# Expert units of eight jobs in one order through the change of jobs, with gather and scatter placed among the units

## The chip, the cores and the metric

One core of one Trainium2 chip runs the whole program. The metric is the device time of the slowest (here the only) core in microseconds; what is compared is the median of several runs. PE is TensorE, PEld its weight loads, DVE is VectorE, ACT is ScalarE, POOL is GpSimd, SP is SyncE, which issues the weight loads from memory.

## What is computed

One step of a two-layer encoder over 288 tokens (256 of a prompt, 32 of a sample) with D = 1024. Each layer is a mixer (gated MLP, banded attention, short convolution, merged) and a feed-forward part: dense in layer 0, a mixture of eight experts with top-2 routing in layer 1. The change touches only the mixture and what follows it:

```python
def swiglu(h, w1, w3, w2):
    a = jnp.einsum('...d,df->...f', h, w1)
    g = jnp.einsum('...d,df->...f', h, w3)
    return jnp.einsum('...f,fd->...d', jax.nn.silu(a) * g, w2)

def moe(h, w_router, b_router, w1, w3, w2):
    logits = jnp.einsum('...d,de->...e', h, w_router) + b_router
    top_v, top_i = lax.top_k(logits, TOP_K)          # 2 of 8
    top_w = jax.nn.softmax(top_v, axis=-1)
    combine = jnp.einsum('...k,...ke->...e', top_w, jax.nn.one_hot(top_i, N_EXPERTS))
    return sum(combine[..., e:e+1] * swiglu(h, w1[e], w3[e], w2[e]) for e in range(N_EXPERTS))
```

An expert has an inner width of 3584. A final RMSNorm over the sum follows. All inputs and outputs are float32.

## The kernel before

Every product in full precision is made of three products in the rounded format float32r: with w = w_hi + w_lo and h = h_hi + h_lo, the kernel adds h_hi*w_hi, h_hi*w_lo and h_lo*w_hi. ScalarE makes a high part by a copy with rounding (round_chunk, L873), VectorE the low part by subtraction (low_chunk, L1338). A weight matrix of 128 x 2048 (1 MB) comes by one DMA from SP into one of six slots (expert_ring) and is split in two chunks of 128 x 1024; there are four buffers w_hi and w_lo (CHUNKS = 4). ScalarE may round chunk c when TensorE has used chunk c - 4 (semaphore chunk_used); VectorE follows (rounded), TensorE waits for split; SP loads the next matrix into a slot when both its chunks are split.

The experts run as jobs. A job is one expert with up to 128 of its tokens (SLOT), and in the profiled execution there are eight, so one per expert. A job has 14 units (UNITS) of 256 inner columns. For each unit TensorE does unit_rows (four chunks, 24 matmuls of 128x512, L1682 to L1684; the out tile holds w1 and w3 columns side by side), ScalarE the SiLU of one half (silu_unit, L881), VectorE the product (silu_times_g, L1343), TensorE two transposes of the result (transpose_hidden, L1692), ScalarE and VectorE its high and low part (hid_high L885, hid_low L1347), and TensorE unit_down (two chunks, 12 matmuls, L1708), which adds into the PSUM banks 6 and 7 over all units of a job. The down projection of a unit comes one unit later, behind the next unit's unit_rows, so that SiLU, transposes and splitting are hidden. Only the job's first unit has no down projection in front of its transposes, and the job's last down projection comes right after its own transposes.

At the two ends of a job stand other steps, all in the function job_units of each engine. Ahead of unit 0, two matmuls with a column of zeros clear banks 6 and 7 (L1720). Behind the last down projection TensorE makes three transposes of the weighted one-hot matrix (L1739), then gather (L1662) for the next job: 24 matmuls of float32 that pick the next job's tokens out of h_tok by the one-hot matrix spread, in tiles of 128, 128 and 32 tokens (a float32 matmul stands as two passes in the trace). ScalarE and VectorE take high and low part of it (L720, L1353), which the next unit_rows needs. ScalarE copies the sums to y_tok (L933), and the scatter follows: eight float32 matmuls of 288 columns (L1747) whose results VectorE adds to x (L1414). These steps use a rotation of the PSUM banks 0 to 5. While they run, ScalarE and VectorE split only the first four chunks of the next job, since there are four buffers.

The order on each engine is written out by hand; there is no scheduler. The loop over the jobs (Fori) covers all but the last one, which is written out again; in it a loop over turns of two units covers twelve of the fourteen. VectorE loads two expert numbers into registers at the loop's head. The end of the program is the last scatter, the squares of x, mean(4), root and norm, and the output DMA from POOL.

## Times and profile before

| | us |
|---|---|
| median of three runs | 1971.55 |
| lowest, highest | 1969.06, 1981.17 |
| profiled execution: its device time | 1977.98 |
| profiled execution: span of its instructions | 1976.2 |
| PE busy in the span | 1882.6 (95%) |
| DVE busy | 1440.9 (73%) |
| ACT busy | 1170.9 (59%) |
| mean granted TensorE clock | 0.976 |
| first expert matmul to last down matmul of job 7 | 869.97 to 1951.36 |

Busy time of PE counts pipelined matmuls whose ends are modelled, each longer than the distance to the next, so 95% doesn't say that PE is at its peak: the distance between starts says more. A row of the timeline gives start, length, engine, line, operation, tiles, shapes and count, and in brackets how long the engine was idle ahead of it and which instruction ended that. Register and branch instructions are in no row.

### The profile page before, as it was taken

How to read it: one execution, taken by the hardware profiler on the slowest of the kernel's cores; microseconds unless marked ns; L12 is line 12 of the kernel's file. 1: busy time of each engine (PE TensorE's matmuls, PEld its weight loads, DVE VectorE, ACT ScalarE, POOL GpSimd, SP SyncE). 2: the span in 40 equal slices, each digit the busy share in tenths (PEclk: the TensorE clock that was granted, in tenths of full speed). 3: DMA queues.
4: the chain of work that ended last, by engine and by line, in shares of the span. 5: the costliest groups of instructions: out<-in, count | busy, mean ns of one | idle time of the engine just before them, and what ended most of it. 6: DMA issues, size and time to landing. Idle time of an engine off the chain costs nothing.

```text
span 1976.2 us, 31336 instructions
## 1 busy us (share of the span) xinstructions
PE 1882.6 (95%) x10698; PEld 1653.7 (84%) x10698; DVE 1440.9 (73%) x1909; ACT 1170.9 (59%) x1522; POOL 19.7 (1%) x39
## 2 busy tenths in 40 slices
PE   7999998999899999889999999999999999999996
PEld 6999998999799999768878778778788787787785
DVE  5563565666655645459979979789799799798896
ACT  4453434333436344348868768678688587686784
POOL 1000000000000000000000000000000000000000
PEclk8999999999999999979999999999999999999999
DMA  7444543444344344329969969879799699698792
GB/s 281 142 161 147 180 162 110 169 152 174 126 162 142 112 146 167 132 87 373 363 240 373 365 236 374 307 291 368 262 361 375 231 373 371 232 372 330 290 371 85
DMA packets 67991, 478.95 MB, mean 242 GB/s; under 512 B 7840, under 2 KB 8864, under 8 KB 10704
## 3 DMA queue, kind: packets, MB, share of 16 engines
q1 hardware_dynamic: 65168, 467.82, 63.4%
q0 software_dynamic: 2608, 10.08, 1.5%
q8 instruction: 51, 0.84, 0.2%
q14 instruction: 20, 0.16, 0.0%
q10 hardware_dynamic: 144, 0.04, 0.0%
HBM read 474.23 MB, written 3.69 MB: 242 GB/s over the span
## 4 chain that ended last, share of the span: by engine, by line
issue 67%; PE 29%; DVE 2%; ACT 1%; DMA 0%; POOL 0%; SPq 0%; ACTq 0%; POOLq 0%; DVEq 0%
PE psum L1584 9%; PE psum L1586 9%; PE psum L1585 9%; DVE h L976 1%; DMA ring<-in_w_in 0%; PE psum L1464 0%; PE psum L1463 0%; DVE rstd L973 0%; DVE w_lo L986 0%; PE psum L1483 0%; ACT w_hi L686 0%; PE psum L1453 0%; DVE attn L1154 0%; PE psum L1525 0%; ACT L716 0%
## 5 line engine op out<-in xcount | busy, mean ns | idle before, releaser
L1338 DVE TENSOR_TENSOR w_lo<-ring,w_hi 128x1024 fp32r<-128x1024 f32 x448 | 543.4, 1224 | 71.5 <-ACT w_hi L873 47.0
L873 ACT ACTIVATE w_hi<-ring 128x1024 fp32r<-128x1024 f32 x448 | 476.1, 1065 | 116.6 <-PE psum L1684 83.5
L986 DVE TENSOR_TENSOR w_lo<-ring,w_hi 128x1024 fp32r<-128x1024 f32 x218 | 266.5, 1224 | 268.1 <-ACT w_hi L686 268.1
L686 ACT ACTIVATE w_hi<-ring 128x1024 fp32r<-128x1024 f32 x218 | 230.9, 1061 | 380.2 <-PE psum L1586 378.5
L1584 PE MATMUL psum<-h_hi,w_hi 128*128 128x288 f32 x1312 | 395.9, 302 | 33.7 <-DVE h_lo L992 22.9
L1585 PE MATMUL psum<-h_lo,w_hi 128*128 128x288 f32 x1312 | 390.8, 298 | 0.0
L1586 PE MATMUL psum<-h_hi,w_lo 128*128 128x288 f32 x1312 | 389.4, 297 | 0.0
L1682 PE MATMUL psum<-w_hi,h_hi 128*128 128x512 f32 x896 | 365.0, 407 | 0.8 <-issue 0.2
L1684 PE MATMUL psum<-w_hi,h_lo 128*128 128x512 f32 x896 | 354.5, 396 | 0.0
L1683 PE MATMUL psum<-w_lo,h_hi 128*128 128x512 f32 x896 | 353.8, 395 | 0.0
L1338 DVE TENSOR_TENSOR w_lo<-spare,w_hi 128x1024 fp32r<-128x1024 f32 x224 | 274.0, 1225 | 24.3 <-ACT w_hi L873 6.0
L1584 PEld LDWEIGHTS psum<-h_hi,w_hi 128*128 128x128 f32 x1312 | 249.4, 190 | 40.9 <-issue 33.9
L873 ACT ACTIVATE w_hi<-spare 128x1024 fp32r<-128x1024 f32 x224 | 237.8, 1062 | 66.5 <-PE psum L1684 66.5
L1586 PEld LDWEIGHTS psum<-h_hi,w_lo 128*128 128x128 f32 x1312 | 250.4, 191 | 0.0
L1585 PEld LDWEIGHTS psum<-h_lo,w_hi 128*128 128x128 f32 x1312 | 250.0, 191 | 0.0
L1682 PEld LDWEIGHTS psum<-w_hi,h_hi 128*128 128x128 f32 x896 | 171.3, 191 | 38.6 <-issue 6.3
L1684 PEld LDWEIGHTS psum<-w_hi,h_lo 128*128 128x128 f32 x896 | 170.9, 191 | 37.4
L1683 PEld LDWEIGHTS psum<-w_lo,h_hi 128*128 128x128 f32 x896 | 171.8, 192 | 33.0
L1708 PE MATMUL psum<-w_hi,hid_hi 128*128 128x512 f32 x448 | 138.9, 391 | 8.1 <-DVE hid_lo L1347 8.1
L1708 PE MATMUL psum<-w_hi,hid_lo 128*128 128x512 f32 x448 | 138.3, 390 | 0.0
L1708 PE MATMUL psum<-w_lo,hid_hi 128*128 128x512 f32 x448 | 138.1, 390 | 0.0
L1708 PEld LDWEIGHTS psum<-w_hi,hid_hi 128*128 128x128 f32 x448 | 83.5, 188 | 26.7 <-issue 9.9
(230 smaller groups left out, 1959.5 us busy)
## 6 DMA issues: line engine op xcount, KB each, us to landing
ring<-in_e_w SPq DMA_DIRECT2D x224, 1024.0 KB, 4.9
spare<-in_e_w SPq DMA_DIRECT2D x112, 1024.0 KB, 4.8
ring<-in_w_in SPq DMA_DIRECT2D x56, 1024.0 KB, 4.9
ring<-in_w SPq DMA_DIRECT2D x33, 1024.0 KB, 4.8
ring<-in_w_branch SPq DMA_DIRECT2D x12, 1024.0 KB, 4.8
ring<-in_w_out SPq DMA_DIRECT2D x8, 1024.0 KB, 4.8
bias<-in_bias_t POOLq DMA_DIRECT2D x2, 1024.0 KB, 9.9
x<-in_x_t SPq DMA_DIRECT2D x4, 288.0 KB, 3.8
```

The lines of the kernel that those rows point to most:

```text
L686: nc.scalar.activation(dst, src, ACT.Copy).then_inc(rounded, 1)
L873: nc.scalar.activation(w_hi[buf][:, :], expert_ring[s][:, half * CHUNK_W:(half + 1) * CHUNK_W], ACT.Copy).then_inc(rounded, 1)
L976: ins = nc.vector.scalar_tensor_tensor(out=h[:, k, :], in0=x[:, k, :], scalar=vec[:, gain + k:gain + k + 1], in1=rstd[:, :], op0=ALU.mult, ...
L986: nc.vector.tensor_tensor(low, src, high.bitcast(f32), ALU.subtract).then_inc(split, 1)
L1338: nc.vector.tensor_tensor(w_lo[buf][:, :], expert_ring[s][:, half * CHUNK_W:(half + 1) * CHUNK_W], w_hi[buf][:, :].bitcast(f32), ALU.subtr ...
L1584: nc.tensor.matmul(bank(name), high, high_src[k], start=(k == 0), stop=False)
L1585: nc.tensor.matmul(bank(name), high, low_src[k], start=False, stop=False)
L1586: ins = nc.tensor.matmul(bank(name), low, high_src[k], start=False, stop=(k == tiles - 1))
L1682: nc.tensor.matmul(out, he_hi[:, k, :], w_high, start=(k == 0), stop=False)
L1683: nc.tensor.matmul(out, he_hi[:, k, :], w_low, start=False, stop=False)
L1684: ins = nc.tensor.matmul(out, he_lo[:, k, :], w_high, start=False, stop=(k == DT - 1))
L1708: ins = nc.tensor.matmul(psum[:, 6 + hf, :], h_part[:, b, :], w_part[:, hf * 512:(hf + 1) * 512], start=False, stop=(last and h_part is hi ...
```

## The change

It takes effect from the end of the routing on. The parts:

- **One order through the change of jobs.** Each matrix stream is now w13, w13, w2 for every unit, with w2 being that of the unit before (np.roll), the one of the last unit wrapping to the front of the next job. Turns are of two units, seven per job; the first two and the last are written out, four run in a loop. In turn 0 of a job TensorE does unit_rows(0), then unit_down of the job before. Job 0 and the last job are written out; the very last down projection stands behind the loops.
- **Gather in the last turn.** In the last turn, after the transposes of unit 12 and ahead of unit_rows of unit 13, TensorE gathers for the next job, from h_tok_hi into banks 4 and 5 and from h_tok_lo into banks 0 and 2, in float32r: 48 matmuls in place of 24 in float32. ScalarE and VectorE copy them to he_hi and he_lo after unit_rows of unit 13. VectorE makes h_tok_lo once, ahead of job 0 (six instructions), and TensorE waits for it.
- **Scatter in four pairs.** ScalarE scales the sums by the token weights while it rounds them (sums_high), VectorE makes the low part (sums_low), both in turn 0 of the next job. The eight rows are scattered in pairs in float32r, 16 matmuls: rows 0, 1 and 2, 3 and 4, 5 and 6, 7 at four places of turns 0 and 1, each pair through banks 4 and 5, with the addition to x on VectorE between its chunks.
- **Weights.** The one-hot matrix is turned unweighted in turn 1 (turn_spread), with three one-column matmuls for the weight of each slot. wspread, its six VectorE operations and the clearing matmuls go.
- **PSUM banks** are fixed: gated 0, 1; transposed 2, 3; 4 and 5 for the rest; sums 6, 7, cleared by start=True at the job's first down projection.

```diff
 TensorE
-            def job_units(job, is_last):
-                pe.wait_ge(he_ready, job * 2 + 2)
-                for hf in range(2):
-                    nc.tensor.matmul(psum[:, 6 + hf, :], zero_col[:, :], he_hi[0:1, 0:4, :], start=True, stop=False)
-                unit_rows("first", 0)
-                transpose_hidden("first")
-                with pe.Fori(0, TURNS) as i:
...
-                unit_rows("last", JOB_MATRICES - 4)
-                unit_down("next", JOB_MATRICES - 2)
-                transpose_hidden("last")
-                unit_down("last", JOB_MATRICES - 1)
...
-                gather("gather", 1 if is_last else 4)
...
+            def gather(after):
...
+                for source, banks in ((h_tok_hi, GATHER_HI), (h_tok_lo, GATHER_LO)):
+                    for hf in range(2):
+                        if after and source is h_tok_lo:
+                            pe.wait_ge(*((e_prod_ready, turns.unit(0)), (e_lo_ready, turns.unit(0)))[hf])
+                        for j in range(4):
+                            at = (4 * hf + j) * P
+                            for n, (t0, rows) in enumerate(TILES):
+                                ins = nc.tensor.matmul(psum[:, banks[hf], j * P:(j + 1) * P], source[0:rows, n, at:at + P],
+                                                       spread[0:rows, n, :], start=(n == 0), stop=(n == 2))
+            def scatter(*rows):
...
+                for j in rows:
+                    if j >= 2:
+                        pe.wait_ge(x_ready, turns.value(MIXER_SUMS + j - 1 - DT * back, DT))
+                    out, cols = psum[:, SPARE[j % 2], 0:TOK], slice(j * P, (j + 1) * P)
+                    nc.tensor.matmul(out, y_hi[:, cols], spread_t, start=True, stop=False)
+                    nc.tensor.matmul(out, y_lo[:, cols], spread_t, start=False, stop=True).then_inc(scattered, 1)
+            def turn_work(t, last=False):
...
+                if t == 1 and boundary:
+                    scatter(2, 3)
+                unit_rows(0)
+                if boundary or t:
+                    unit_down(4, 1, last=(t == 0))
+                turn_hidden(0)
+                if t == TURNS - 1 and not last:
+                    gather(1)
+                if t == 1 and boundary:
+                    scatter(4, 5)
+                unit_rows(1)
+                if t < 2 and boundary:
+                    scatter(*((0, 1) if t == 0 else (6, 7)))
+                unit_down(10, 0, first=(t == 0))
+                turn_hidden(1)
+                if t == 1:
+                    turn_spread()
 VectorE
+            def turn_work(t, e, following=None, last=False):
...
+                if t == 1 and boundary:
+                    add_rows(2, 3)
+                if not (turns.first and t == 0):
+                    low_chunks(4, 5)
+                low_chunks(6)
+                silu_times_g(0)
+                low_chunks(7, 8, 9)
+                if t == 0:
+                    if boundary:
+                        sums_low()
+                    nc.vector.tensor_copy(wsel[:, :], weight[:, :, bass.ds(e, 1)].rearrange("p n o -> p (n o)")
+                                          ).then_inc(wsel_ready, 1)
+                hidden_low(0)
+                if t == 1 and boundary:
+                    add_rows(4, 5)
+                low_chunks(10, 11)
+                if not last:
+                    low_chunks(12)
+                if t == TURNS - 1 and not last:
+                    gathered_low(0, 1)
+                silu_times_g(1)
+                if t == TURNS - 1 and not last:
+                    gathered_low(1, 1)
+                if not last:
+                    low_chunks(13)
+                if boundary and t < 2:
+                    add_rows(*((0, 1) if t == 0 else (6, 7)))
+                if not last:
+                    low_chunks(14, 15)
+                hidden_low(1)
+                if t == 1:
+                    turned_spread()
+                    if following:
+                        hot_rows(*following)
...
+            with dve.Fori(1, last_job) as job:
+                turns.job = job
+                job_work(expert_of(job), (job + 1, expert_of(job + 1)))
 ScalarE
+            def turn_work(t, last=False):
...
+                round_chunks(7, 8, 9)
+                if t == 0 and not turns.first:
+                    sums_high()
+                hidden_high(0)
...
+                silu_unit(1)
+                if t == TURNS - 1 and not last:
+                    gathered_high(1)
```

## Rows read from the trace of the kernel before

**Rows 1.** Windows: stretch, its length, busy PE/PEld/DVE/ACT/POOL, PEclk, DMA share, GB/s

```profile
1145.00:1282.00 137.00, 133.91 (x602) 108.23 (x602) 118.25 (x133) 101.78 (x118) 0.00 (x0) 0.99 0.85 321
1190.00:1198.40 8.40, 8.40 (x39) 6.93 (x38) 7.92 (x10) 6.93 (x8) 0.00 (x0) 1.00 1.00 376
```

**Rows 2.** Timeline of PE: starts of job 0, its end, two clearings, the last end

```profile
869.97 0.79 PE L1682 MATMUL psum<-w_hi,h_hi 128*128 128x512 f32 x1
...
995.76 0.56 PE L1739 MATMUL psum<-ident,pt 128*128 128x128 f32 x3
...
1145.88 0.73 PE L1720 MATMUL psum<-h_hi,zero_col 1*128 1x512 f32 x2
...
1283.02 0.73 PE L1720 MATMUL psum<-h_hi,zero_col 1*128 1x512 f32 x2
...
1951.36 0.56 PE L1739 MATMUL psum<-ident,pt 128*128 128x128 f32 x3
```

**Rows 3.** Timeline of PE: hidden transposes, five units apart

```profile
1181.56 0.38 PE L1692 MATMUL psum<-ident,h 128*128 128x128 f32 x2
...
1223.67 0.38 PE L1692 MATMUL psum<-ident,h 128*128 128x128 f32 x2
```

**Rows 4.** Timeline of PE: the last down projection, turned weights, gather, scatter

```profile
1267.15 0.72 PE L1708 MATMUL psum<-w_hi,hid_hi 128*128 128x512 f32 x2 [1.01 <-DVE hid_lo L1347]
...
1270.01 0.56 PE L1739 MATMUL psum<-ident,pt 128*128 128x128 f32 x3
1270.50 8.51 PE L1662 MATMUL psum<-a_t,rows 128*128 128x128 f32 x48
1278.94 4.15 PE L1747 MATMUL psum<-c_t,bias 128*128 128x288 f32 x16
```

**Rows 5.** Around the first unit's transposes: timelines of ACT and PE, a window

```profile
1289.19 1.28 ACT L881 ACT_TABLE_LOAD   x1
...
1291.38 0.69 PE L1692 MATMUL psum<-ident,h 128*128 128x128 f32 x2 [1.95 <-DVE h L1343]
...
1291.90:1294.60 2.70, 2.70 (x7) 2.15 (x7) 2.70 (x8) 0.38 (x1) 0.00 (x0) 0.50 0.74 261
```

**Rows 6.** Timeline of PE: neighbours in the rounded format, 288 columns

```profile
500.03 0.29 PE L1586 MATMUL psum<-hid_hi,w_lo 128*128 128x288 f32 x1
500.16 0.30 PE L1584 MATMUL psum<-hid_hi,w_hi 128*128 128x288 f32 x1
```

**Rows 7.** Timeline of PE inside the gather: passes on 32 rows, then on 128

```profile
1271.14 0.48 PE L1662 MATMUL psum<-a_t,rows 32*128 32x128 f32 x2
...
1271.77 0.50 PE L1662 MATMUL psum<-a_t,rows 128*128 128x128 f32 x3
```

**Rows 8.** Groups by line: weight loads of rounded and of float32 matmuls

```profile
L1708 PEld LDWEIGHTS psum<-w_lo,hid_hi 128*128 128x128 f32 x448 | 84.1, 188 | 17.5
...
L1662 PEld LDWEIGHTS psum<-a_t,rows 128*128 128x128 f32 (+1 forms) x396 | 53.7, 188 | 16.1 <-ACT rows L720 1.0
```

**Rows 9.** Timelines of DVE and ACT: chunks, low parts, sums, x, hot rows

```profile
859.83 4.63 DVE L1338 TENSOR_TENSOR w_lo<-ring,w_hi 128x1024 fp32r<-128x1024 f32 x4 [1.71 <-ACT w_hi L873]
...
1266.59 0.42 DVE L1347 TENSOR_TENSOR hid_lo<-psum,hid_hi 128x256 fp32r<-128x256 f32 x1 [0.76 <-ACT hid_hi L885]
...
1270.21 1.08 ACT L933 ACTIVATE bias<-psum 128x512 f32<-128x512 f32 x2 [0.32 <-PE psum L1708]
...
1275.45 0.69 DVE L1353 TENSOR_TENSOR h_lo<-psum,h_hi 128x512 fp32r<-128x512 f32 x1 [1.96 <-ACT h_hi L720]
...
1280.28 3.30 DVE L1414 TENSOR_TENSOR x<-x,psum 128x288 f32<-128x288 f32 x8
1286.48 3.95 DVE L1338 TENSOR_TENSOR w_lo<-ring,w_hi 128x1024 fp32r<-128x1024 f32 x3 [2.90 <-ACT w_hi L873]
...
1293.32 0.84 DVE L1331 TENSOR_SCALAR a_t<-slot_id,job_base,place 128x128 f32<-128x128 f32 x3
```

**Rows 10.** Timeline of PE: the gather of job 0

```profile
858.90 8.51 PE L1662 MATMUL psum<-a_t,rows 128*128 128x128 f32 x48 [0.68 <-ACT rows L720]
```

More of the change, by code:

```diff
@@ L197, in add @@
             self.at[n] = (b, self.total, list(self.last[b]))
[L198 removed]
+            self.last[b] = [n]
             self.total += counted([n])
[L201 to L210 removed]
 def number_groups():
@@ new lines, in round_chunks, with silu_unit @@
+            def round_chunks(*chunks):
+                at = turns.turn
+                for c in chunks:
+                    round_chunk(c)
+                    turns.turn = at
+            def silu_unit(odd):
+                act.wait_ge(chunk_used, turns.chunk(9 if odd else 3))
+                if not (turns.first and turns.turn == 0 and not odd):
+                    act.wait_ge(e_prod_ready, turns.unit(odd, 1))
+                nc.scalar.activation(e_silu, psum[:, GATED[odd], 0:UNIT], ACT.Silu).then_inc(e_silu_ready, 1)
@@ L1677, in unit_rows, with split_chunk @@
+            def split_chunk(c):
+                pe.wait_ge(split, turns.chunk(c))
+                return w_hi[turns.buffer(c)], w_lo[turns.buffer(c)]
+            def unit_rows(odd):
+                if turns.turn or not turns.first:
+                    pe.wait_ge(e_prod_ready, turns.unit(odd, 2))
+                out = psum[:, GATED[odd], :]
                 for part in range(4):
-                    hi, lo = split_chunk(at + part // 2, part % 2, in_turn)
+                    hi, lo = split_chunk(6 * odd + part)
@@ new lines, in turn_work @@
+            def turn_work(t, last=False):
+                turns.turn = t
+                boundary = not turns.first
+                if t == 1 and boundary:
[15 more added lines that the diff above has]
+                    turn_spread()
@@ new lines, in job_work @@
+            def job_work(last=False):
+                pe.wait_ge(he_hi_ready, turns.value(2, 2))
+                pe.wait_ge(he_lo_ready, turns.value(2, 2))
+                for t in range(PEELED):
+                    turn_work(t)
+                with pe.Fori(0, TURNS - PEELED - 1) as i:
+                    turns.i = i
+                    turn_work(PEELED)
+                    turns.i = None
+                turn_work(TURNS - 1, last)
+            gather(0)
+            job_work()
+            turns.first = False
@@ L1755, in _ @@
+            unit_down(4, 1, last=True)
+            scatter(*range(DT))
             mean(4)
```

602 lines of the change are left out of this document (265 added, 337 removed).

## The prediction

> **What bounds the kernel now.** First the windows, to see which engine has room. In one expert job of the kernel before, TensorE is busy for nearly all of 137 us, VectorE for 118, ScalarE for 102, and the loads run at 321 GB/s; inside a job they run at 376 GB/s with the DMA engines at share 1.00 [rows 1]. Busy time of TensorE says little, so the second view is where its instructions start. Jobs repeat every 1283.02 - 1145.88 = 137.14 us [rows 2]. Inside a job the hidden transposes of successive units stand (1223.67 - 1181.56)/5 = 8.42 us apart [rows 3], with no wait between. Fourteen units at that pace are 117.9 us, so each job loses 19.2 us at its two ends, and eight jobs have about 154 us of it. All that the change can win lies there.
>
> The order of time at one change of jobs shows where it lies [rows 4]. The last down projection waits 1.0 us for its own hidden rows. It is over at 1270.01, and then come three transposes (0.5 us), the gather (8.4 us), the scatter (4.1 us) and the clearing of the sums (0.7 us, rows 2): 13.7 us without an expert matmul. The other 5.5 us are inside the job: 137.1 - 117.9 - 13.7. They come from the first unit, which has no down projection to hide its SiLU behind: TensorE sits idle for 1.95 us, and in the stretch after that its granted clock is 0.50, the 1.2 GHz level, for some 2.7 us [rows 5].
>
> **The pieces, one by one.**
>
> *Steady units.* The new turn has the same order on every engine (two down chunks, four gated chunks, SiLU after the third, high part after the sixth), so its pace stays 8.42 us: 112 units are 943.0 us.
>
> *First and last unit.* Job 0 still starts without a down projection. It took 995.76 - 869.97 = 125.8 us to its last down matmul [rows 2], 7.9 more than 117.9; 1.3 of that is the wait before the last down projection (1.0 and the restart), which now stands only at the end of job 7. So 7.9 us stay, once. Between jobs both vanish: the last down projection runs behind the next job's first unit. The matmuls with zeros go.
>
> *Gather.* It had 24 fp32 matmuls of 128 columns in two passes, 8.4 us. It gets 48 matmuls in the rounded format (24 on the high part, 24 on the low). Their price is not in the trace, since every rounded matmul there has 288 or 512 columns: at 288 they start 0.13 us apart [rows 6], with 288/2.4 GHz = 0.12. The fp32 passes of the gather tell what 128 columns cost [rows 7]: passes on the same 128 rows start 0.11 us apart ((0.50 - 0.27)/2), but around each tile of 32 rows the gaps are 0.21 ((1271.77 - 1271.14)/3). Four gaps in six are of that kind, as if the load there came after the pass before and not under it. An fp32 pass streams two cycles a column (128 columns 0.107), so the load is about 0.1 too. A rounded matmul here has 0.053 of streaming and 0.107 of load, and in the pattern 128, 128, 32 rows with one pass each, every one sits beside a change of rows: 0.16 us each, 48 make 7.7 us. From below, with loads hidden, 128/2.4 GHz + 0.013 (what 288 columns take over 0.12) = 0.067 each, 3.2 us. From above, each as dear as the fp32 one: twice 8.44, 16.9 us. I take 7.7.
>
> Weight loads have the same duration in the two formats, 188 ns [rows 8], which speaks against the lower end. The Trainium skill, "TensorE: Matmul & The Clock Gate", section "Weight-path perf modes — Fast Weight Load (FWL) and DoubleRow", says that a full load of 128 weights takes a faster path when the input type isn't FP32. If the rounded type counted as such, the gather would be 3.2 us and not 7.7, and the result that of rival 1; the trace, with equal loads, does not agree.
>
> The gather lies behind nothing: it goes in whole on TensorE. Its evacuations lie beside the down projection of 12 x 0.227 = 2.7 us: ScalarE has 2 x 0.5 us for the high part, VectorE 2 x 0.7 us for the low one, between chunk 12 and the product (the old subtraction took 0.69, rows 9). They are ready after about 2.6 us, before the next job's rows ask for them at 3.0, so no stall; were both engines late by a chunk, 1.1 us.
>
> *Scatter.* 16 rounded matmuls of 288 columns at 0.13 = 2.1 us, instead of 4.1.
>
> *Turned weights.* Three transposes 0.5 us [rows 4], plus three fp32 matmuls of one column, six passes bounded by 0.11 and 0.21 [rows 7]: 0.9. Together 1.4 us in each of eight jobs.
>
> *The wait this brings.* VectorE now splits chunks straight through the boundary. Between them it carries sums_low (2 x 0.7), eight row additions (3.30 for eight), hot_rows (0.8) and three small copies (0.7 together, an estimate from the 0.69 of a 512-column one) [rows 9]. Back to back it needs (4.63 - 1.22)/3 = 1.14 us a chunk, and 0.4 each for product and hidden low part: 7.6 us a unit against 8.42. Over a whole job it has room (14 x 7.6 + 8 = 114 us), but not in turn 0.
>
> I follow that turn, with zero at the first matmul of the new job's unit 0. VectorE's hidden_low of the last unit comes at 3.1 (the gathered parts, then three chunks at 1.14). Then stands the loop's head with two value loads, which are in no row; before, VectorE was free from 1283.58 to 1286.48 and was released by ScalarE [rows 9], so the head costs 0 to 2.9 us. I take 1.5, the middle. Chunk 4 starts at 4.5 and is split at 5.8, where TensorE wants it at 5.5: 0.4 lost. VectorE then has ten chunks (4 to 13), two products, sums_low, wsel and hidden_low: 11.4 + 0.8 + 1.4 + 0.1 + 0.4 = 14.1, to 18.6, and rows 0 and 1 at 19.0 and 19.4. TensorE needs rows, down, transposes, rows, scatter(0, 1), down and transposes: 5.5 + 0.4 + 2.7 + 0.2 + 5.5 + 0.5 + 2.7 + 0.2 = 17.7, with 0.1 before down(10), whose chunk is queued behind sums_low. So scatter(2, 3), which waits for rows 0 and 1 to leave their banks, is 1.4 late; add_rows(0, 1) is queued behind chunk 13, and everything later of TensorE behind the scatter. Turn 1 repeats this with more room, 0.3 at turn_spread, which waits for row 7. With 0.3 for restarts that is 2.5 us per boundary. The bounds: 0.5, if the head costs nothing and the four chunk buffers take up the rest; 6, if the head costs 2.9 and one activation table is reloaded on ScalarE ahead of the rounding, as now (1.28, rows 5).
>
> *Loads.* The SP queue issues the same 42 matrices per job into the same six slots, w2 of the last unit now among the next job's. Each is asked for when its slot's second chunk is split, as before, so POOL's queue is passed by nothing. 42 x 1.049 MB = 44.0 MB at 376 GB/s are 117 us, under the 131.6 that a job will have: hidden.
>
> *Start.* VectorE makes six low parts of h_tok (6 x 0.65 = 3.9 us) before TensorE may gather, which started at 858.90 [rows 10]; so it starts 3 us later. It is 0.8 shorter, and what follows it (0.6 + 0.7 + zeros 1.2, to 869.97) shrinks by 1.6. TensorE is then idle for 3.7 us, so part of the gather may run at 1.2 GHz, as the matmuls after the idle time of rows 5 did: 0.7 (nothing to 4). Together +1.3.
>
> *End.* Before: turned weights, gather 2.1, scatter 4.1. After: high and low sums exposed (0.3 + 0.5 + 2 x 0.7 = 2.2), then eight rows through two banks, the addition of 0.41 being the pace with its waits, about 0.5 us each. 6.6 before against 6.2 after: taken as nothing.
>
> **The sum**, from the first expert matmul to the last down matmul: 943.0 + 7.9 + 7 x (7.7 + 2.1 + 2.5) + 8 x 1.4 = 1048.2 us. Before, the same stretch is 1951.36 - 869.97 = 1081.4 [rows 2]: -33.2, with the start -31.9. The profiled execution has a span of 1976.2 us inside a time of 1977.98; it would become a span of 1944. The median of the runs is 1971.55, so the prediction is 1971.55 - 31.9 = 1940 us.
>
> **Rivals.**
> 1. *Cheaper boundary.* If weight loads hide behind the short matmuls, the gather is 3.2 and the sum 8 x 4.5 = 36 less, 1904; if besides only the stalls shrink to 0.5, 7 x 2.0 = 14 less, 1926, still the forecast. For it: passes on the same rows do start 0.11 apart. Against it: the gaps around the 32-row tile [rows 7] and the equal loads [rows 8]. 0.05 for 1904, 0.05 for something between it and 1924. The Trainium skill's rule on fast loads, named above, would make it the first.
> 2. *VectorE becomes the bound at the boundary.* 6 us of stalls instead of 2.5: 7 x 3.5 = 24.5 more, 1964. For it: VectorE has 0.8 us of room per unit, and in the four units of turns 0 and 1 it gets 6.5 us of extra work. 0.14.
> 3. *The gain is not there.* Loads were at share 1.00 inside a job, and each boundary gave them a rest. If a backlog makes slots late, the wait moves to ScalarE's rounding; some 4.5 us a boundary take all back: 1971. Against it: the mean need is 44.0 MB in 131.6 us, 335 GB/s. 0.07.
> 4. *Slower: short rounded matmuls cost as fp32 ones.* 0.35 us each on the path: 8 x 9.2 = 74 more, 2014. It decides from 7.7 + 31.9/8 = 11.7 us a gather, 0.24 us a matmul. Against it: the 0.13 at 288 columns. For it: nothing in the trace has a narrow one. 0.12, and 0.02 for other losses.
>
> The forecast, 1924 to 1955, keeps 0.55. A measurement of this kernel can tell about 1% from no change, 1952 to 1991. Faster: 0.55 + 0.10 = 0.65; within 1%: rivals 2 and 3, 0.21; slower: 0.14. The range runs from 1912 (half of rival 1 left out, 0.05) to 1975 (rival 4 and the rest left out, 0.14).
>
> **What would show it.** Hidden transposes 8.42 us apart inside jobs, unchanged; the period of jobs 131.6 us; the gather 7.7 us from its first to its last start, with gaps of 0.16; no half clock except at the start; TensorE's waits at scatter(2, 3) on VectorE's x, about 1 us, and nowhere on the ring. A gather over 11 us, or ScalarE waiting for DMA, would make it wrong.

## The result: slower, and the profile after

The changed kernel takes 2001.22 us (median of 4 runs, 2001.04 to 2001.93) against 1970.3 us for the kernel before, taken beside it (4 runs, 1969.06 to 1981.17): a ratio of 1.0145, with an interval from 1.0109 to 1.0182. The forecast was 1940 us with a range to 1975, so both the number and the direction were wrong.

Windows of the changed kernel: stretch, its length, busy PE/PEld/DVE/ACT/POOL, granted clock of TensorE, DMA share, GB/s. The first answers to the long one of [rows 1], the next five follow one change of jobs, the last two are the gather of the start.

```profile
1147.00:1283.80 136.80, 136.55 (x606) 111.27 (x605) 116.55 (x130) 98.21 (x116) 0.00 (x0) 0.96 0.85 322
...
1269.40:1274.40 5.00, 5.00 (x28) 3.87 (x26) 2.75 (x4) 1.33 (x2) 0.00 (x0) 1.00 0.96 365
1274.40:1282.10 7.70, 7.70 (x26) 5.91 (x25) 0.00 (x0) 0.00 (x0) 0.00 (x0) 0.54 0.25 104
1282.10:1284.10 2.00, 2.00 (x6) 1.61 (x6) 0.00 (x0) 0.00 (x0) 0.00 (x0) 0.50 0.00 0
1284.10:1286.00 1.90, 1.90 (x8) 1.49 (x7) 0.00 (x0) 0.94 (x1) 0.00 (x0) 0.68 0.00 0
1286.00:1291.90 5.90, 5.90 (x28) 4.82 (x27) 5.25 (x7) 4.79 (x8) 0.00 (x0) 1.00 0.28 85
...
865.50:873.70 8.20, 8.18 (x25) 6.30 (x25) 4.50 (x4) 1.71 (x3) 0.00 (x0) 0.50 0.57 218
873.70:882.00 8.30, 8.21 (x25) 6.25 (x24) 0.75 (x2) 0.60 (x1) 0.00 (x0) 0.50 0.39 164
```

TensorE is now busy for 136.55 of 136.80 us: the idle 1.95 us of [rows 5] and the wait of [rows 4] are gone, as the change means. But the granted clock fell from 0.99 to 0.96 over the job. It is 1.00 in the first half of the gather, and then 0.54, the lower level of 1.2 GHz for nearly all of 7.7 us, and 0.50 for two more us of expert matmuls. The rows of the timeline below follow one another without an idle stretch, so this is not the fall after a wait that [rows 5] had. All seven changes of jobs have it, for 10.2 us at four and 13.7 us at three.

Timeline of TensorE around the same change of jobs: start, us, instruction, count, idle time before it. L1698 are the hidden transposes that [rows 3] follows, L1669 the gather, L1723 the scatter's high matmuls.

```profile
1269.30 0.38 PE L1698 MATMUL psum<-ident,h 128*128 128x128 f32 x2
1269.43 5.01 PE L1669 MATMUL psum<-bm_lo,h_tok_hi 128*128 128x128 f32 x24
1274.37 7.79 PE L1669 MATMUL psum<-bm_lo,h_tok_lo 128*128 128x128 f32 x24
1282.10 0.80 PE L1688 MATMUL psum<-w_hi,h_hi 128*128 128x512 f32 x1
...
1291.89 0.38 PE L1698 MATMUL psum<-ident,h 128*128 128x128 f32 x2
...
1310.12 0.40 PE L1723 MATMUL psum<-bm_hi,ac_hi 128*128 128x288 f32 x1 [0.25 <-DVE x L1353]
...
1338.73 0.38 PE L1698 MATMUL psum<-ident,h 128*128 128x128 f32 x2
...
1406.09 0.38 PE L1698 MATMUL psum<-ident,h 128*128 128x128 f32 x2
```

Two hidden transposes with nothing between them but a unit stand 8.42 us apart. Here they stand 1291.89 - 1269.30 = 22.59 us apart, so a gather adds 14.17 us, itself (12.67) and what runs slowly behind it. In the old order it took 8.44 ([rows 4], 1270.50 to 1278.94). The period is 1406.09 - 1269.30 = 136.79 us; without the gather, 122.6. The five units after the gather take 1338.73 - 1291.89 = 46.84, 4.74 more than five at 8.42: scatter, turned weights and all stalls together.

Where the 23.1 us between the spans (1976.2 and 1999.3) lie, from the starts below and those of [rows 2, 10]:

```profile
841.73 3.58 PE L1627 MATMUL psum<-rw,h 128*128 128x8 f32 x16 [6.20 <-DVE h L948]
...
865.52 8.23 PE L1669 MATMUL psum<-bm_lo,h_tok_hi 128*128 128x128 f32 x24 [3.32 <-DVE h_tok_lo L1415]
...
882.74 0.77 PE L1688 MATMUL psum<-w_hi,h_hi 128*128 128x512 f32 x1 [0.83 <-issue]
...
1967.79 1.08 PE L1708 MATMUL psum<-w_hi,hid_hi 128*128 128x512 f32 x2 [2.68 <-DVE w_lo L1313]
...
1974.76 0.55 PE L1723 MATMUL psum<-bm_hi,ac_hi 128*128 128x288 f32 x1 [2.39 <-DVE ac_lo L1343]
```

The router's matmuls (L1627) start at 841.73, after code that the change leaves alone; before, they started at 837.92. These 3.8 us differ from execution to execution: over all profiles below that start lies between 833.4 and 841.8. From there to the first expert matmul it is 41.0 us (before 32.0): +9.0. The expert stretch to the end of the last down projection, at 1972.2, is 1089.5 (before 1081.4): +8.1. What follows is 27.1 (before 24.8): +2.3.

### The profile page after: what moved, and what is told of

Its sections match the earlier page's. It is cut to its first block, busy times and chain, and to the rows that moved or that the text cites. A ratio compares the mean times of both kernels' runs of the same rounds, so it can differ in the third digit from the quotient of the medians.

```text
span 1999.3 us, 30646 instructions
## 1 busy us (share of the span) xinstructions
PE 1917.8 (96%) x10718; PEld 1688.5 (84%) x10718; DVE 1430.9 (72%) x1894; ACT 1145.8 (57%) x1507; POOL 19.8 (1%) x39
## 4 chain that ended last, share of the span: by engine, by line
issue 67%; PE 29%; DVE 2%; ACT 1%; DMA 0%; POOL 0%; SPq 0%; ACTq 0%; POOLq 0%; DVEq 0%
PE psum L1584 9%; PE psum L1585 9%; PE psum L1586 9%; DVE h L948 1%; DMA ring<-in_w_in 0%; PE psum L1464 0%; PE psum L1463 0%; DVE rstd L945 0%; DVE w_lo L958 0%; PE psum L1483 0%; ACT w_hi L660 0%; PE psum L1453 0%; DVE attn L1126 0%; PE psum L1525 0%; ACT L689 0%
## 5 line engine op out<-in xcount | busy, mean ns | idle before, releaser
L1313 DVE TENSOR_TENSOR w_lo<-ring,w_hi 128x1024 fp32r<-128x1024 f32 x448 | 540.9, 1223 | 45.0 <-ACT w_hi L843 17.4
L1313 DVE TENSOR_TENSOR w_lo<-spare,w_hi 128x1024 fp32r<-128x1024 f32 x224 | 271.5, 1223 | 112.1 <-ACT w_hi L843 109.6
```

The lines of the kernel that those rows point to most:

```text
L1313: nc.vector.tensor_tensor(w_lo[buf][:, :], expert_ring[s][:, c % 2 * CHUNK_W:(c % 2 + 1) * CHUNK_W], w_hi[buf][:, :].bitcast(f32), ALU.sub ...
```

## The experiments

All kernels but the last of this table are the changed kernel with an edit of its gather. "Gather" is the distance of the hidden transposes around it less 8.42 us, "rest" the period without it, both read at one change of jobs; ratios stand with their interval. The times are medians of four runs, of two in rows three and four (256 columns, in two places) and of ten for the padded rounded kernel twice over.

```
kernel                         gather, us added   period   rest    time, median   ratio to before
changed kernel                 14.17              136.8    122.6   2001.2         1.0145
float32 gather                 8.44               131.1    122.6   1942.4         0.982 (0.979-0.986)
256 columns, 36 of 48          17.03              139.7    122.6   2014.4         1.019 (1.015-1.022)
in two places                  6.50 + 8.18        137.3    122.6   2007.8         1.015 (1.012-1.019)
high part alone, 24            6.54               129.2    122.7   1926.9         0.977 (0.973-0.981)
12 of 48                       3.41               126.1    122.7   1924.2         0.975 (0.971-0.979)
tiles grouped                  8.09               130.8    122.7   1951.7         0.988 (0.985-0.991)
padded, rounded                5.36               128.1    122.8   1925.6         0.976 (0.972-0.980)
padded, rounded, twice         10.71              133.5    122.8   1973.9         0.999 (0.997-1.001)
padded, float32                5.35               128.0    122.6   1916.1         0.970 (0.967-0.974)
swapped                        4.49               126.9    122.4   1917.0         0.970 (0.967-0.973)
swapped, twice                 8.07               130.5    122.4   1946.5         0.986 (0.982-0.990)
swapped, padded                3.70               126.1    122.4   1905.3         0.965 (0.962-0.969)
old order, padded float32      -                  134.0    -       1950.4         0.988 (0.985-0.991)
```

The column "rest" is the finding of the table: whatever the gather costs, 122.4 to 122.8 us of the period remain. The new order is worth what was forecast, and most of the miss lies in the gather.

One change of jobs stands for all seven only where the clock stays up: there the seven agree within 0.02 us. Where it falls, the length of the fall differs. The gather adds 14.1 to 15.7 us in the changed kernel, 17.0 to 17.2 with 256 columns, 14.7 to 16.4 (both halves) in two places, 5.0 to 7.9 with the high part alone, 3.4 to 6.5 with 12 and 8.0 to 9.7 with the tiles grouped.

**The gather in float32 again.**

```diff
-for source, banks in ((h_tok_hi, GATHER_HI), (h_tok_lo, GATHER_LO)):
+for source, banks in ((h_tok_hi, GATHER_HI),):      # h_tok in float32
...
-    tensor_copy(he_lo, psum[GATHER_LO[hf]])
+    tensor_tensor(he_lo, psum[GATHER_HI[hf]], he_hi, subtract)
```

> The changed kernel with one part undone: the gather is 24 float32 matmuls again (h_tok kept whole, no h_tok_lo, VectorE subtracts the high part as before); order of units, scatter in pairs and everything else stay. Theory A (the short rounded matmuls are the loss: 0.21 us each at 2.4 GHz and the granted clock falls to 0.50 under them, 14.2 us per change of jobs): gather 8.4 us at clock 1.00, no stretch at 0.50 at a change of jobs, period of jobs 136.8 - 14.2 + 8.5 = 131.1 us, start some 10 us earlier, time about 1950. Rival B (the new order with VectorE and ScalarE working through the change of jobs is the loss, whatever the format): period stays above 136, time 1990 or more.

Timeline of TensorE, transposes L1691 and gather L1662:

```profile
1370.31 0.38 PE L1691 MATMUL psum<-ident,h 128*128 128x128 f32 x2
1370.52 8.41 PE L1662 MATMUL psum<-bm_lo,h_tok_hi 128*128 128x128 f32 x48
1387.17 0.38 PE L1691 MATMUL psum<-ident,h 128*128 128x128 f32 x2
```

The period is 131.1 us and the time 1942.4 us, 34 us less than the kernel before beside it (1976.8). No change of jobs shows the lower clock. So order, scatter and stalls give the forecast's gain, and the rounded format takes it back.

**A wider moving operand.** 36 of the 48 matmuls stream 256 columns instead of 128, the loads are the same.

```diff
-psum[:, banks[hf], j * P:(j + 1) * P], source[...], spread[0:rows, n, :]
+psum[:, banks[hf], j * P:j * P + w], source[...], spread[0:rows, n, 0:w]   # w = 256 for j < 3
```

> The changed kernel with the one-hot matrix 256 columns wide (128 more slots, whose results are overwritten) in three of four groups of the gather, so 36 of 48 rounded matmuls stream 256 columns in place of 128; the result is the same. Theory A1 (the price of a short one is its weight load of 0.107, not hidden, plus its streaming): 256 columns cost 0.05 more each, the gather gets longer by 1.9 us at 2.4 GHz, time 2001 to 2020. Theory A2 (a rounded matmul is dearer below some width, and cheap above it as the 0.13 at 288 columns): matmuls on 128 rows start 0.12 apart, gather 8 to 9 us with the clock at 1.00 for longer, time about 1965.

```profile
1275.40 5.92 PE L1669 MATMUL psum<-bm_lo,h_tok_hi 128*128 128x256 f32 x24
1281.25 9.11 PE L1669 MATMUL psum<-bm_lo,h_tok_lo 128*128 128x256 f32 x23
```

The high half takes 5.85 us instead of 4.94: 0.9 for 18 wide ones, 0.05 each, which is what 128 columns more take at 2.4 GHz. So in this gather a load and the stream behind it add up; had the load been the longer of two that overlap, the columns would have been free. The clock falls as in the changed kernel, for 13.7 us at every change of jobs.

**The gather in two places**, the low half ahead of the last turn's first unit and the high one where it was.

```diff
+if t == TURNS - 1 and not last:
+    gather(1, ("low",))
 unit_rows(0)
...
-    gather(1)
+    gather(1, ("high",))
```

> The changed kernel with its gather in two stretches: the low part stands at the start of the last turn (banks 4 and 5), the high part stays after the transposes of unit 12 (banks 0 and 2), so 24 short matmuls, 36 long ones, 24 short ones. Nothing is left out. Theory C1 (the clock falls because the short matmuls go on for more than the first 5 us): both stretches take 5.0 us at 1.00, the 8 slow matmuls after them vanish, period 136.8 - 4.3 = 132.5, time about 1971. Theory C2 (the clock falls at any such stretch, only late): each stretch is followed by slow matmuls of some 2 us, period 136 or more, time about 2000.

The transposes stand 14.92 and 16.60 us apart around the two halves: 6.50 and 8.18 us; at four of the seven changes of jobs it is 7.9 and 8.3. A half-clock stretch of 3.4 or 6.8 us follows the first half and one of 6.8 us the second. Splitting doesn't help: the clock falls behind each half of 24, and two falls cost at least what one longer one did.

**Only the high part**, and **a quarter of the groups**: how much of it brings the clock down. The second leaves out three quarters of the gathered rows.

```diff
-for source, banks in ((h_tok_hi, GATHER_HI), (h_tok_lo, GATHER_LO)):
+for source, banks in ((h_tok_hi, GATHER_HI),):      # h_tok_hi rounded
```

> The changed kernel with only the high part of the rows gathered, in the rounded format: 24 short matmuls instead of 48 (the low part of the gathered rows is left out, so is the low part of the tokens in token order at the start). In the changed kernel the first 24 take 4.94 us at a granted clock of 1.00 and the clock falls to 0.50 only when they are done. Theory H1 (what lowers the clock is a stretch of such matmuls as soon as there are a few us of them, and the bill comes after it): the 24 take 4.9 us, then one stretch of some 3.4 us at half clock, in which 1.7 us of work is lost; gather 6.6 us, period 122.6 + 6.6 = 129.2 us, time near 1940 us. Theory H2 (24 are too few to lower it): no stretch at half clock at a change of jobs, gather 4.9 us, period 127.5 us, time near 1928 us.

```diff
-for j in range(4):
+for j in range(1 if after else 4):
```

> The changed kernel with one group of 128 features of four gathered in each half at the changes of jobs: 12 short rounded matmuls instead of 48 (three quarters of the gathered rows are left out after the first job). 12 x 0.206 = 2.5 us at full clock. By H1 with no lower limit on their number: one stretch of 3.4 us at half clock behind it, 2.5 + 1.7 = 4.2 us, period 126.8 us, time near 1931 us. By H2: no half clock, period 125.1 us, time near 1919 us. Either way it gives the price of the order without a gather: period less the gather should be the 122.6 us that the changed kernel and the one with the float32 gather give.

Windows of the high part's stretch behind its gather, then of the quarter's gather and what follows it:

```profile
1366.50:1373.30 6.80, 6.80 (x24) 5.45 (x24) 2.36 (x2) 2.97 (x3) 0.00 (x0) 0.75 0.27 112
```

```profile
1242.80:1246.30 3.50, 2.64 (x16) 2.00 (x14) 2.72 (x4) 1.33 (x2) 0.00 (x0) 1.00 0.92 351
1246.30:1254.50 8.20, 8.20 (x37) 6.72 (x38) 5.24 (x7) 5.72 (x8) 0.00 (x0) 1.00 0.62 231
```

With 24 matmuls (5 us) a stretch of 3.4 us at half clock follows six of seven gathers (6.8 at one), and 6.54 us are added, 1.6 more than the matmuls take: theory H1, predicted period 129.2, measured 129.2. The time, 1926.9 us, is below the 1940 forecast for it and near the 1928 of H2: the start, without low parts to wait for, is 12 us shorter too, so here the period decides and not the time. With 12 the clock stays up in five of seven gathers and falls, for 3.4 and 6.8 us, in two; so neither H1 without a lower limit nor H2 holds as it stands, and the time, 1924.2, is above the 1919 of H2. There the low matmuls must wait 0.86 us for hidden rows, a cover that the longer gather gave: 3.41 us for 2.5 us of matmuls.

**The third tile padded to 128 rows**, with zeros.

```diff
+nc.vector.memset(h_tok_hi[:, 2, :], 0.0); nc.vector.memset(h_tok_lo[:, 2, :], 0.0)
...
-source[0:rows, n, at:at + P], spread[0:rows, n, :]
+source[:, n, at:at + P], spread[:, n, :]
```

VectorE also writes the one-hot tile on all 128 rows, which is not shown here.

> The changed kernel with the gather's third token tile padded with zero rows from 32 to 128, so that all 48 matmuls have 128 rows (two memsets more before the gather of the start; nothing left out). In the changed kernel, at full clock, a matmul after one of the same 128 rows starts 0.164 us behind it, the 32-row one 0.206 and the next 128-row one 0.250 behind. Theory K1 (the change of the number of rows costs the rest): all 0.164 us apart, 24 high ones in 3.9 to 4.0 us instead of 4.94; gather shorter by 1.0 us at full clock and up to 2 with the rest of it at half clock; period 135 to 136 us, time 1985 to 1995 us. Theory K2 (the 0.25 belongs to the beginning of a new sum in PSUM): it stays at 4.9 us and the time at 2001 us.

First four neighbours in the high half of the changed kernel's gather, each on its own, which show what a change costs there: their starts are 0.16, 0.21 and 0.25 us apart. Then the timeline of TensorE in the padded kernel and the window of its gather:

```profile
1270.65 0.33 PE L1669 MATMUL psum<-bm_lo,h_tok_hi 128*128 128x128 f32 x1
1270.82 0.28 PE L1669 MATMUL psum<-bm_lo,h_tok_hi 128*128 128x128 f32 x1
1271.02 0.32 PE L1669 MATMUL psum<-bm_lo,h_tok_hi 32*128 32x128 f32 x1
1271.27 0.33 PE L1669 MATMUL psum<-bm_lo,h_tok_hi 128*128 128x128 f32 x1
```

```profile
1239.17 0.38 PE L1702 MATMUL psum<-ident,h 128*128 128x128 f32 x2
1239.31 2.88 PE L1673 MATMUL psum<-bm_lo,h_tok_hi 128*128 128x128 f32 x24
1242.02 2.84 PE L1673 MATMUL psum<-bm_lo,h_tok_lo 128*128 128x128 f32 x24
1252.95 0.38 PE L1702 MATMUL psum<-ident,h 128*128 128x128 f32 x2
```

```profile
1367.40:1372.90 5.50, 5.50 (x52) 5.50 (x51) 2.74 (x4) 1.33 (x2) 0.00 (x0) 1.00 0.97 380
```

This was the surprise: both theories were far too timid. 24 matmuls take 1242.02 - 1239.31 = 2.71 us, 0.113 each instead of 0.206, and the clock doesn't fall at any change of jobs. The gather adds 5.36 us instead of 14.17, and one edit of two memsets and a few slices turns 2001.2 us into 1925.6. PEld, the weight load, is busy for all 5.50 us of the window, in the changed kernel for 3.87 of 5.00: now loads follow one another without a break, which points to the load as what bounds the matmul. Even two matmuls on the same 128 rows, 0.164 apart in the mix, are at 0.113 when no 32-row one is near.

**The same in float32, and in the old kernel.** The slices and the memset alone, in the kernel with the float32 gather and in the kernel before the change.

```diff
-h_tok[0:rows, n, at:at + P], spread[0:rows, n, :]
+h_tok[:, n, at:at + P], spread[:, n, :]
```

> The changed kernel with the gather in float32 again (24 matmuls) and its third token tile padded with zero rows to 128; nothing left out. The float32 gather with the 32-row tile added 8.44 us, 0.35 a matmul; the padded rounded one took 0.113 a matmul where the mixed one took 0.206. Theory P1 (a mix of 128-row and 32-row matmuls is what costs, in either format): 24 float32 matmuls at about twice 0.113 = 5.4 us, period 131.1 - 3.0 = 128.1 us, time 1942 - 8 x 3.0 = 1918 us. Theory P2 (only the rounded format pays for the mix): 8.4 us and 1942 us as before.

> The kernel before the change, in its old order and with its float32 gather, with nothing but the third token tile padded to 128 rows; nothing left out. It tells whether the price of the mixed row counts was in the old kernel too. P1: seven gathers of 24 matmuls and that of the start fall from 8.4 to 5.4 us: 8 x 3.0 = 24 us, time 1973 - 24 = 1949 us, period 134.1 us. P2: no change, 1973 us.

The last two starts are the gather and the scatter of the old kernel, padded, which answer to [rows 4]; ahead of them the gather of the float32 one.

```profile
1230.22 0.38 PE L1694 MATMUL psum<-ident,h 128*128 128x128 f32 x2
1230.44 5.52 PE L1665 MATMUL psum<-bm_lo,h_tok_hi 128*128 128x128 f32 x48
1243.99 0.38 PE L1694 MATMUL psum<-ident,h 128*128 128x128 f32 x2
```

```profile
1259.49 5.62 PE L1665 MATMUL psum<-a_t,rows 128*128 128x128 f32 x48
1264.95 4.05 PE L1750 MATMUL psum<-c_t,bias 128*128 128x288 f32 x16
```

P1 holds in both: 1264.95 - 1259.49 = 5.46 us instead of 8.44, the period 134.0 instead of 137.1, the times 1916.1 (expected 1918) and 1950.4 (expected 1949). In the old kernel the clock also falls in fewer first units of a job, at three changes instead of five, and periods without the fall are 132.4 us. The kernel before carried this cost all along, and its own rows told it: the gaps of 0.21 around the 32-row tile in [rows 7]. Padded, a float32 gather of 24 matmuls in two passes (5.35 us) costs the same as a rounded one of 48 (5.36). So the format gains nothing at 128 columns, where a pass takes the same 0.11 us in either format. The 9.5 us between the two, 1916.1 against 1925.6, lie at the start: from the router to the first hidden transposes the float32 kernel takes 34.1 us and the rounded one 43.6, which waits 4.21 us for the low parts and then runs its gather at half clock.

**Tiles grouped**, four matmuls of one tile after another, no padding. The start flag stands only at the first matmul of a bank and the stop flag at its last.

```diff
-for j in range(4):
-    for n, (t0, rows) in enumerate(TILES):
+for n, (t0, rows) in enumerate(TILES):
+    for j in range(4):
```

> The changed kernel with the 12 matmuls of each half of the gather in another order: four of the first token tile, four of the second, four of the 32-row one, instead of tile by tile for each group; nothing padded or left out. The number of changes between 128 and 32 rows falls from 32 to 8 in a gather. Theory K1 (each change of the row count costs): 40 x 0.113 + 8 x 0.24 = 6.4 us or less for 48 instead of some 10 at full clock, no fall of the clock or a short one, period about 129 us, time 1930 to 1940 us. Theory K3 (each 32-row matmul costs, whatever its neighbours): (0.164 + 0.206 + 0.250 - 2 x 0.113) = 0.39 us for each of 16, total as now, time near 2000 us.

```profile
1383.46 3.30 PE L1669 MATMUL psum<-bm_lo,h_tok_hi 128*128 128x128 f32 x24
1386.69 4.02 PE L1669 MATMUL psum<-bm_lo,h_tok_lo 128*128 128x128 f32 x24
```

```profile
1383.50:1386.70 3.20, 3.20 (x27) 2.92 (x25) 2.67 (x3) 1.33 (x2) 0.00 (x0) 1.00 0.91 353
1386.70:1390.70 4.00, 4.00 (x26) 3.63 (x25) 0.00 (x0) 0.00 (x0) 0.00 (x0) 0.79 0.92 375
1390.70:1396.00 5.30, 5.30 (x14) 4.18 (x14) 1.23 (x1) 1.06 (x1) 0.00 (x0) 0.52 0.00 0
```

At full clock 24 take 3.23 us, 0.135 each, so three quarters of the surplus over 0.113 went with three quarters of the changes (8 left of 32): K1, each change of the row count costs. One by one, the starts around a change stand 0.20 us apart into it and 0.16 for the next matmul, on the new row count already, and 0.11 from there on: 0.14 us more for a change. (The fewer start flags aren't the reason: the padded kernel keeps all of them at 0.113.) The 16 changes of 24 matmuls in the changed kernel are then 2.2 us, which is the whole of 4.94 - 2.71. But the clock still falls, for 6.8 us at four changes of jobs (as here, 9.6 us added) and 3.4 at three (8.09, the row of the table), and the time of 1951.7 us is above K1's 1930 to 1940 for that reason.

**Operands swapped**, so that the one-hot matrix is loaded and the token rows stream in 512 columns: 12 matmuls instead of 48, then a copy and eight transposes.

```diff
-psum[:, banks[hf], j * P:(j + 1) * P], source[0:rows, n, at:at + P], spread[0:rows, n, :]
+psum[:, SPARE[hf], :], spread[0:rows, n, :], source[0:rows, n, hf * 512:(hf + 1) * 512]
...
+nc.tensor.transpose(psum[:, SPARE[k // 4], ...], g_tok[:, k * P:(k + 1) * P], ident)   # eight
```

> The changed kernel with the gather's operands changed about: the one-hot matrix is the stationary one and 512 columns of h_tok_hi or h_tok_lo stream, 12 rounded matmuls into banks 4 and 5 in place of 48; the rows of slots are copied to SBUF under unit_rows of unit 13, turned by eight transposes ahead of its down projection, and split as before. Nothing is left out. Theory A: 12 x 0.23 and some for the 32-row tile = 3.0 us, eight transposes 0.9, clock at 1.00, period 136.8 - 14.2 + 3.9 = 126.5, start 12 us earlier, time about 1917. Rival B (waits at the change of jobs decide): the transposes wait for the copies and the next job's rows for both parts, period above 131, time above 1945.

Timeline of TensorE: a few of the 12, on 128 and on 32 rows, and the transposes.

```profile
1364.10 0.40 PE L1679 MATMUL psum<-h_tok_hi,bm_lo 128*128 128x512 f32 x1
1364.34 0.39 PE L1679 MATMUL psum<-h_tok_lo,bm_lo 128*128 128x512 f32 x1
1364.66 0.50 PE L1679 MATMUL psum<-h_tok_hi,bm_lo 32*128 32x512 f32 x1
1365.00 0.39 PE L1679 MATMUL psum<-h_tok_lo,bm_lo 32*128 32x512 f32 x1
...
1372.69 1.04 PE L1689 MATMUL psum<-ident,bias 128*128 128x128 f32 x8
```

1917.0 us, as expected. The change of rows costs here too: 0.24 us between equal ones, 0.32 into a change and 0.34 for the one behind it, 0.18 us more in all. But there are only four in a gather, and the clock stays up.

**Two doublings** ask whether the clock stays up in these kernels only since their gathers are short. Each computes every sum twice over.

```diff
-for n, (t0, rows) in enumerate(TILES):
+for again, (n, (t0, rows)) in [(a, t) for a in range(2) for t in enumerate(TILES)]:
```

> The kernel with the operands of the gather swapped (token rows stream 512 wide, 12 matmuls, 3.6 us, no fall of the clock), with each of its two halves computed twice over: 24 matmuls, about 7.2 us, nothing left out. It is longer than the 24 short high matmuls (4.9 us) after which the changed kernel's clock falls. Theory S1 (it is the short matmuls, not rounded work of this length, that lower the clock): 3.6 us more for each gather and no half clock, period 126.9 + 3.6 = 130.5 us, time 1917 + 8 x 3.6 = 1946 us. Theory S2 (any rounded gather of over 5 us lowers it): one stretch or more at half clock, 1.7 us more each, period 132.2 us and more, time 1960 us and more.

> The kernel with the rounded gather padded to 128 rows everywhere, with each sum computed twice over: 96 short rounded matmuls on end, some 10.8 us at 0.113 each instead of 5.4; nothing left out. The mixed gather let the clock fall behind its first 24 (4.9 us), the grouped one behind some 30 (4 us), the padded one of 48 (5.4 us) not at all. Theory L1 (it is the mix of 128 and 32 rows, which leaves gaps between short matmuls, that lets the clock fall): granted clock 1.00 through all 10.8 us, 8 x 5.4 us more than the 1925.6 us of the padded one, so 1969 us. Theory L2 (short rounded matmuls lower it once there are enough of them on end, mixed or not): a fall in or behind each gather, of at least one stretch of 3.4 us at 0.50, 1.7 us lost in each and up to 5: 1982 to 2008 us.

The window of the second, over its whole gather and over the unit's matmuls behind it:

```profile
1260.30:1271.10 10.80, 10.80 (x99) 10.80 (x98) 2.67 (x3) 1.33 (x2) 0.00 (x0) 1.00 0.59 238
1271.10:1279.00 7.90, 7.90 (x36) 6.54 (x36) 4.98 (x6) 5.46 (x8) 0.00 (x0) 1.00 0.16 51
```

The clock stays at 1.00 in both, through 7.1 us of 512-column matmuls and through 96 short ones in 10.8 us: S1 and L1. It is not the length, nor short rounded matmuls as such. It is short rounded ones with 32-row ones among them; whether the 32 rows or the changes count for the clock no run separates, and the grouped order, with a quarter of the changes, still had the fall. The periods are 130.5 (expected 130.5) and 133.5; the time of the second, 1973.9, is 5 us above the forecast of 1969, with the start's gather doubled at the lower clock there (10.2 us more to the first hidden transposes, not 5.4). That start also limits the finding: once the clock is down, after a wait of 4.19 us, 96 equal matmuls don't bring it up. It is 0.50 through all 20 us of them.

**Swapped, padded, high part first.**

```diff
-for hf in range(2):
-    for n, (t0, rows) in enumerate(TILES):
-        for source in (h_tok_hi, h_tok_lo):
+for source in (h_tok_hi, h_tok_lo):      # at the start, wait for htok_low only ahead of the low ones
+    for hf in range(2):
+        for n in range(3):               # all of 128 rows
```

> The kernel with the swapped gather, its third tile padded to 128 rows, and the high matmuls ahead of the low ones, so that at the start the high ones need not wait for the low part of the tokens; nothing left out. The 0.32 to 0.34 us at a change of the row count should fall to the 0.24 of equal ones: 12 x 0.235 = 2.8 us instead of 3.6, so 0.8 us less in a period of 126.9, i.e. 126.1. At the start the gather can begin 4 us earlier and then waits for the low part: 1.5 us, and up to 5 if TensorE's clock then stays at its upper level through the start (20 us at 0.50 there now). Time 1917 - 8 x 0.8 - (1.5 to 5) = 1906 to 1909 us. If the mix has no price here: 1912 to 1915 us.

```profile
856.87 1.66 PE L1685 MATMUL psum<-h_tok_hi,bm_lo 128*128 128x512 f32 x6 [0.68 <-ACT h_tok_hi L696]
859.70 1.66 PE L1685 MATMUL psum<-h_tok_lo,bm_lo 128*128 128x512 f32 x6 [1.16 <-DVE h_tok_lo L1432]
...
1358.49 0.38 PE L1725 MATMUL psum<-ident,h 128*128 128x128 f32 x2
1358.62 1.65 PE L1685 MATMUL psum<-h_tok_hi,bm_lo 128*128 128x512 f32 x6
...
1370.61 0.38 PE L1725 MATMUL psum<-ident,h 128*128 128x128 f32 x2
```

1905.3 us, the fastest: 0.965 of the kernel before. The gather adds 3.70 us instead of the 4.49 of the swapped one, and from the router's matmuls to the first hidden transposes it takes 41.0 us instead of 46.1. With the start's gather inside the second figure, 1917.0 - 7 x 0.8 - 5.0 = 1906.4.

## Why the prediction was wrong

*What held.* The unit pace of 8.42 us inside jobs. Period less gather: the forecast had 123.9 (117.9 + 2.1 + 2.5 + 1.4), measured 122.6. Within it, scatter, turned weights and stalls were put at 6.0 us and take 4.7. The stalls were most likely the part oversized: at 2.5 forecast, they are 1.2 by difference if the other two hold, and TensorE waits 0.25 us at scatter(2, 3), where 1.4 were worked out, with the middle taken for a loop head that no row showed. Rival 2 needed the opposite. The loads stayed hidden (share 0.85 over the job, no wait on the ring): rival 3 is out. The float32 gather (1942.4 us) is the forecast's time reached with the gather at 8.4 instead of 7.7.

*The step that failed* is "0.16 us each, 48 make 7.7 us". It has two terms.
1. The price. At full clock the 24 high ones took 4.94 us, 0.206 each: 9.9 us for 48, 2.2 above the term. The reading of [rows 7] was right, a load beside a change of rows isn't hidden, but 0.16 was load and stream added up without anything for the change itself. The gap between the two 128-row ones is indeed that sum, the other two are longer. The gaps were 0.164 on equal rows, 0.206 to the 32-row one and 0.250 after it. What [rows 7] offered and I passed over is the other reading: the changes themselves are what costs, so take them away. Padded, 0.113.
2. The clock, which was not in the sum at all. 14.17 - 9.9 = 4.3 us per change of jobs is work at 1.2 GHz, in the second half of the gather and the first rows of the next unit. The prediction said "no half clock except at the start"; its rows had the fall only after idle time ([rows 5]).

Together 14.17 instead of 7.7, seven times 6.5 = 45 us. Three of the seven lost more: read one by one the gathers add 103.4 us, 14.8 in the mean, and that is 49.5 above seven times 7.7. Against it stands 7 x 1.3 = 9 for the rest: 1048.2 + 49.5 - 9 = 1089, measured 1089.5.

*Rival 4* had the outcome on its side of the line, which it drew at 11.7 us a gather, and a chance of 0.12. Its mechanism was not the one, so the outcome on its side is luck: it priced a rounded matmul as a float32 one, 0.35, and that isn't what happened in the mix (0.206 at full clock). *Rival 1* put the short matmul at 0.067, loads hidden; without any change of rows it is 0.113. The Trainium skill, "TensorE: Matmul & The Clock Gate", section "Weight-path perf modes — Fast Weight Load (FWL) and DoubleRow", gives a full load a faster path when the type isn't FP32. The padded kernels don't agree for the rounded type: 0.113 a matmul in it and 5.46 / 48 = 0.114 a pass in float32. The same page of the Trainium skill, section "LDWEIGHTS (loading the stationary operand)", says that the load goes with the columns at 1.2 per ns and not with the rows, which gives an estimate of 107 ns for 128; the 0.113 between starts on equal rows agrees with it.

*Start.* Put at +1.3, it is +9.0. The later beginning was right: 2.8 us (forecast 3). The gather then ran wholly at 0.50, 16.5 us instead of 8.4; the forecast allowed 0.7 for that, and "nothing to 4". The fall came with the wait of 3.32 us ahead of the gather. That the wait matters is supported by the last kernel, where the high part doesn't wait: half clock there is 6.8 us instead of 20.5, and 5.0 us are won, of which some belong to the shorter gather. Padding alone doesn't do it: the padded rounded kernel still waits, and has 17.1 us at half clock there.

*End.* Put at nothing, it is +2.3, besides a wait of 2.68 us ahead of the last down projection. There the chunks come late (w_lo L1313), and behind it the low sums (2.39 us). No run changes either, so their cause is not shown.

*What stays open.* That at a change of jobs the fall of the clock needs short rounded matmuls and 32-row ones in one chain is shown by what fell and what didn't; what the chip measures is not, nor why 12 matmuls bring the fall at two changes of seven. The 3.8 us before the router are left to the execution: I did not find a cause, and the other profiles spread by twice that.

## What to carry to other kernels

Where tiles of 128 rows and a short last tile alternate in a chain of short matmuls, pad the last one with zeros: here it took a gather from 8.4 to 5.5 us in float32 and from 14.2 to 5.4 in the rounded format. The rounded format gains nothing at 128 columns, where a pass costs the same in either; streaming the wide operand, 512 columns to a load, does: 3.7 us added instead of 5.4, both padded. A new shape of matmul on the critical path is to be priced by a run of that shape: the order here was forecast well, and a price put together from another format, with no term for the clock, undid it.

## What the runs showed of the hardware

- Rounded matmuls with a load each, 2.4 GHz, start to start: 128 columns 0.113 us on equal rows without a break; with every third on 32 rows 0.164, 0.206 to the 32-row one, 0.250 behind it. At 512 columns 0.24, then 0.32 into a change of rows and 0.34 behind it. One change costs 0.14 us at 128 columns and 0.18 at 512.
- The granted clock can fall to 0.50 with TensorE busy for the whole stretch by the profile: after 24 rounded matmuls of 128 or 256 columns in a mix of 128 and 32 rows (4.9 to 5.9 us; at one change of seven it did not in the kernel with 24 alone), in the second half of the grouped order, and at two changes of seven around 12. At the changes of jobs it did not fall in 96 equal ones (10.8 us), in 24 of 512 columns with the mix (7.1 us), or in the float32 gather with the mix (8.4 us). Already at 0.50, at the start, it did not rise during 96 equal ones (20 us) or 24 of 512 columns (12.6 us).
